# Hybrid decoder trunk: pooled projection in f32 with f32 band matmuls, x work as fine queued steps, SiLU phase moved up

## Chip, cores and metric

One Trainium2 chip, the program on all 8 cores, each with two of the 16 sequences. The time is the device time of the slowest core in microseconds (us), lower is better.

## Reference

```python
for l in range(2):                                  # x: (16, 2048, 1024) f32
    z = rms_norm(x, norm1_g[l]) @ w_in[l]           # 1792 columns, split over three mixers
    ya = silu(layer_norm(causal_dwconv31(a * sigmoid(gate)) + b)) @ w_pw[l]          # 384
    yb = u * (tril(w_s) @ layer_norm(v) + b_s)      # gelu, chunks of 128             # 384
    yc = ((trailing means over 2/4/8/16) - z_c) @ w_pool[l] * pool_scale[l]           # 256
    x = x + concat([ya, yb, yc]) @ w_out[l]
    gate, up = split(rms_norm(x, norm2_g[l]) @ w_gate_up[l], 2)                       # 2816 each
    x = x + (silu(gate) * up) @ w_down[l]
out = rms_norm(x, final_g)
```

## The kernel before

A core keeps one sequence of 2048 tokens as `xT`, 1024 features on 8 times 128 partitions, in f32. The tokens are cut into four blocks j of 512. A layer runs, on TensorE: `A` (the gated projection of mixer A, per block 8 groups of 8 matmuls 128x384), `V` and `U` (mixer B's projections), `conv`, then a loop over blocks with `U`, `ZB`, `SP`, `V`, `Z`, `TR`, `PT`, then the SiLU phase (`lnt`: 16 transposes of the normalised convolution output `xc` into a quad of four PSUM banks and four SiLU activations on ScalarE, for each of three channel tiles), then `WO` (output projection) and `FFN`, whose last chunk ends in a down projection of 32 groups of four matmuls 128x512, ordered by block.

The pooled mixer: `Z` projects each 128 tokens to 256 columns, ScalarE copies them scaled to bf16 (`zh`), VectorE writes what the rounding left (`zl`). `ZB` multiplies both with constant band matrices (`band`, `bandp` from the piece before, `bandc` at the sequence's start): for each of four windows six matmuls, seven in block 0. `PT` transposes the result.

Each engine takes its instructions in program order. Background work (norms, statistics, the convolution's Toeplitz tiles `toep`) is held as closures in the queues `bg`, `lo`, `nq` and `hq`; `tick` and `tick_n` pop some of them between foreground groups, and `need(tag)` pops until a tag is done. A norm (`norm_closures`) squares 8 tiles on ScalarE (`sqa`), adds them in pairs on VectorE (`sqr`), sums them on TensorE (`stat`, four matmuls 128x1 with `ocS`), and takes the power on GpSimd. In the kernel before it is six closures, and at the start of a layer also makes `xb`, the bf16 input of the projections. `x_tr` transposes a block of the staged input `xst` into `xT` (32 f32 transposes, 8 copies split over ScalarE and VectorE), and `fin_store` transposes a block back, scales it on VectorE (8 operations into `osA`, `osB` or `osF`) and stores it. Both are foreground code. Between the two sequences, every block goes through norm `rF`, `fin_store`, `x_tr`, norm `r1` and `A`; `pre` in the main loop sets that order.

Of the kernel before, what the change touches and what calls it, by code (L numbers as in the profile page):

```python
# [11 lines left out]
D = 1024  # L12
S = 2048
NT = 512
# [172 lines left out]
def build_program(nseq=2, depth=2):  # L187
# [51 lines left out]
    bt = alloc("bt", [128, 32], F32)  # L239
# [4 lines left out]
    w_pw = alloc("w_pw_sb", [128, 3, DA], BF16)  # L244
# [45 lines left out]
    y2 = AT("y2", 98304, [128, NBLK + 2, NG], BF16)  # L290
    silT = AT("silT", 98304, [128, 3, S], BF16)
# [16 lines left out]
    XSO = [45056, 61440, 77824, 61440]  # L308
    xstage = [[AT("xst%d_%d" % (j, q), XSO[j] + 4096 * q, [128, D], F32) for q in range(4)] for j in range(NJ)]
# [138 lines left out]
    def tick_n(n):  # L448
        for _ in range(n):
            if not hq or not pop_h():  # L450
                break
        if nq:
            pop(nq)
# [25 lines left out]
    def x_dma(s, j, eng="sync"):  # L479
        for q in range(4):  # L480
            tb = 4 * j + q
            dma(eng, xstage[j][q][:], x_d[s, tb * 128:(tb + 1) * 128, :], [], [xstage[j][q].b()])
# [5 lines left out]
    def load_w_rest(s, l):  # L488
# [3 lines left out]
        if s == 0:  # L492
            dma("gpsimd", w_pw[:], w_pw_d[l], [], [B("w_pw")])
# [14 lines left out]
    def load_wo(s, l):  # L508
        ha = [wo_b(0, 0), wo_b(0, 1)]
        hc = [wo_b(1, 0), wo_b(1, 1)]  # L510
        if s == 0:
            dma("gpsimd", woA[:, 0:3, :], w_out_d[l, :, 0:3, :], [], ha)
            dma("sync", wpf[:], w_pool_d[l], [], [wpf.b()])
# [6 lines left out]
    def fuse_a(h):  # L520
        hs = slice(512 * h, 512 * h + 512)
        got = []
        for ci in range(3):
            bk, bb = next_bank()
            mm(bk[:], [(w_pw[:, mk, ci * 128:(ci + 1) * 128], woA[:, mk, hs]) for mk in range(3)],
               [B("w_pw"), wo_b(0, h)], [bb])
# [60 lines left out]
    def band_consts():  # L587
        for g, w in enumerate((2, 4, 8, 16)):
            T = dF[:, 0, :]
# [10 lines left out]
            pool(lambda e: e.iota(bt[:], [[1, 32]], base=1, channel_multiplier=0,  # L600
                                  allow_small_or_imprecise_dtypes=True), [], [bC3])
# [3 lines left out]
            pool(lambda e: e.affine_select(out=bt[:], in_=bt[:], pattern=[[1, 32]], compare_op=ALU.is_ge, fill=0.0,  # L605
                                           base=0, channel_multiplier=-1), [bC3], [bC3])
            vec(lambda e, g=g: e.tensor_copy(out=bandc[:, 0, g, :], in_=bt[:]), [bC3], [bC3])
            tt(bandc[:, 1, g, :], bt[:], bandc[:, 0, g, :], ALU.subtract, [bC3], [bC3])
        pool(lambda e: e.memset(onesF[:], 1.0), [], [bC3])

    sq_rr = [0]

    def norm_closures(s, l, j, rt, kind, with_xb):
# [27 lines left out]
        def mkxb(k):  # L641
            if k % 2 == 0:
# [10 lines left out]
        def step(p):  # L653
            if p >= 2:
                stat(p - 2)
            if p < 4:
                for k in (2 * p, 2 * p + 1):
                    if with_xb:
                        mkxb(k)
                    sq(k)  # L660
            if 1 <= p <= 4:
                add(p - 1)
            if p == 5:
                fin()
        for p in range(6):
# [259 lines left out]
    def zb(tl, i, q):  # L925
        return tl[i].b(q, lo=512 * q, n=512)
# [321 lines left out]
```

How the kernel before makes its waits and increments, by code:

```python
                def body(eh):  # L165
                    for fn, waits, tok, dma in e.ops:
                        for k, v in waits:
                            eh.wait_ge(sems[k], v)
                        ins = fn(eh)
                        ins.then_inc(sems[tok[0]], 16 if dma else 1)
                    if e.name == "sync":
                        for k, v in finals:
                            eh.wait_ge(sems[k], v)
```

## Time and profile before

| | |
|---|---|
| runs | 2943.06 us median of 3 (2941.85 to 2948.37) |
| profiled execution | 2949.38 us, its span 2947.5 us on the slowest core |
| spans of the eight cores | 2935.0 to 2947.5 us |
| TensorE matmul busy | 2754.1 us, 93% of the span |
| VectorE, ScalarE, GpSimd busy | 1234.6, 794.5, 174.0 us |
| TensorE's share of the chain that ended last | 84% |
| an output tile, from issue to landing at the end | 2.9 us |

The busy share is a mean over stages that differ: in the FFN stages TensorE is busy without a gap, and its idle time lies in the start, between the two sequences, in the mixers and at the end. So what a change is worth is read stage by stage.

### The profile page before, as it was taken

The numbers are of one execution on the slowest core, as the hardware profiler recorded it, in microseconds if no ns is written. First come the engines' busy times: TensorE is split into PE (matmuls) and PEld (weight loads), VectorE is DVE, ScalarE is ACT, GpSimd is POOL, SyncE is SP. The second block draws the span as 40 slices with busy tenths as digits, with TensorE's granted clock in tenths as the row PEclk, the third lists the DMA queues.
The fourth block names the chain that finished last, engine by engine and source line by source line (L and its number), as shares of the span: only waits on it lengthen the run. The fifth ranks groups of instructions, "written<-read, shape, count | busy, mean of one in ns | idle before, by whom it ended". The sixth has DMA issues, their size and how long they took to land.

```text
span 2947.5 us, 42647 instructions; the slowest of 8 cores (2935.0 to 2947.5 us)
## 1 busy us (share of the span) xinstructions
PE 2754.1 (93%) x14860; PEld 1395.5 (47%) x14860; DVE 1234.6 (42%) x2256; ACT 794.5 (27%) x1360; POOL 174.0 (6%) x280
## 2 busy tenths in 40 slices
PE   4799999999998999999877899999999989999998
PEld 3554444444465344444455644444445644444444
DVE  2464431323664523323454653323335644323237
ACT  3554201011545311010244532010016442010102
POOL 3010100000000010000000001000000100000000
PEclk8799999999999999999978999999999999999999
DMA  8213342210123072121333026221002121121102
GB/s 189 39 35 58 51 71 51 36 30 15 31 51 69 1 116 36 29 50 22 95 129 76 17 44 93 46 44 36 15 16 54 26 51 36 29 51 36 36 15 115
DMA packets 124031, 150.35 MB, mean 51 GB/s; under 512 B 71728, under 2 KB 98224, under 8 KB 121776
## 3 DMA queue, kind: packets, MB, share of 16 engines
q0 software_dynamic: 36512, 97.33, 19.7%
q1 hardware_dynamic: 87312, 50.31, 6.1%
q8 instruction: 124, 2.03, 0.3%
q14 instruction: 83, 0.68, 0.1%
HBM read 215.05 MB, written 25.69 MB: 82 GB/s over the span
## 4 chain that ended last, share of the span: by engine, by line
PE 84%; DVE 6%; issue 3%; ACT 3%; DMA 2%; POOL 1%; SPq 1%; DVEq 0%; ACTq 0%; POOLq 0%
PE quad L346 78%; PE quad L364 2%; PE quad L793 2%; DVE h2T L397 1%; ACT sqa L375 1%; PE quad L963 1%; DMA yd<-ytok 1%; ACT silT L375 1%; DVE sqr L385 1%; SPq L338 1%; PE quad L787 1%; DVE xT L385 1%; PE quad L636 1%; DVE vg L397 0%; DVE ybt L397 0%
## 5 line engine op out<-in xcount | busy, mean ns | idle before, releaser
L346 PE MATMUL quad<-h2T,ring 128*128 128x512 bf16 x5632 | 1222.6, 379 | 0.0
L346 PEld LDWEIGHTS quad<-h2T,ring 128*128 128x128 bf16 x5632 | 549.7, 98 | 665.0 <-issue 7.7
L385 DVE TENSOR_TENSOR act<-tsil,quad 128x512 bf16<-128x512 f32 x352 | 241.8, 687 | 952.4 <-PE quad L346 932.5
L346 PE MATMUL quad<-act,wd 128*128 128x512 bf16 x2816 | 615.6, 379 | 0.4
L385 DVE TENSOR_TENSOR xT<-xT,quad 128x512 f32<-128x512 f32 x640 | 438.2, 686 | 418.0 <-PE quad L346 391.3
L375 ACT ACTIVATE tsil<-quad 128x512 f32<-128x512 f32 x352 | 210.0, 597 | 1478.1 <-PE quad L346 1466.7
L346 PEld LDWEIGHTS quad<-act,wd 128*128 128x128 bf16 x2816 | 272.4, 98 | 327.1 <-issue 4.1
L375 ACT ACTIVATE sqa<-xT 128x512 bf16<-128x512 f32 x320 | 186.3, 619 | 221.8 <-DVE sqr L385 188.3
L346 PE MATMUL quad<-w_uv_sb,xb 128*128 128x384 bf16 x1024 | 177.8, 333 | 7.4 <-DVE zl L397 6.4
L346 PE MATMUL quad<-w_a_sb,xb 128*128 128x384 bf16 x1024 | 180.7, 338 | 0.1
L346 PEld LDWEIGHTS quad<-w_uv_sb,xb 128*128 128x128 bf16 x1024 | 100.8, 100 | 77.8 <-issue 16.8
L346 PEld LDWEIGHTS quad<-w_a_sb,xb 128*128 128x128 bf16 x1024 | 101.0, 101 | 68.9 <-issue 9.5
L636 PE MATMUL quad<-ocS,sqr 128*128 128x1 bf16 x640 | 38.7, 164 | 94.2 <-DVE sqr L385 93.7
L346 PE MATMUL quad<-silT,woA 128*128 128x512 bf16 x384 | 104.9, 382 | 0.0
L636 PEld LDWEIGHTS quad<-ocS,sqr 128*128 128x128 bf16 x640 | 33.8, 98 | 139.3 <-issue 124.5
L338 POOL DMA_DIRECT2D ring<-w_gate_up x88 | 46.7, 533 | 863.9 <-PE quad L346 799.7
L397 DVE SCALAR_TENSOR_TENSOR h2T<-xT,pv,quad 128x512 bf16<-128x512 f32 x128 | 89.2, 740 | 4.5 <-PE quad L346 4.3
L397 DVE SCALAR_TENSOR_TENSOR ytok<-quad,r,sig 128x384 bf16<-128x384 f32 x64 | 39.5, 618 | 104.4 <-PE quad L346 87.6
L385 DVE TENSOR_TENSOR sqr<-sqa,sqa 128x512 bf16<-128x512 bf16 x160 | 66.7, 419 | 30.4 <-ACT sqa L375 27.3
L346 PE MATMUL quad<-yc,woA 128*128 128x512 bf16 x256 | 77.0, 383 | 0.0
L346 PE MATMUL quad<-ybT,woB 128*128 128x512 bf16 x256 | 76.9, 382 | 0.0
L650 POOL TENSOR_TENSOR r<-r,mhalf 128x4 f32<-128x4 f32 x32 | 32.6, 1017 | 621.3 <-DVE r L391 621.3
(126 smaller groups left out, 1730.8 us busy)
## 6 DMA issues: line engine op xcount, KB each, us to landing
ring<-w_gate_up POOLq DMA_DIRECT2D x88, 512.0 KB, 7.5
wd<-w_down POOLq DMA_DIRECT2D x12, 1536.0 KB, 12.1
xst<-x SPq DMA_DIRECT2D x24, 512.0 KB, 7.4
out<-osF SPq DMA_DIRECT2D x16, 512.0 KB, 2.9
w_a_sb<-w_a POOLq DMA_DIRECT2D x8, 768.0 KB, 23.2
w_uv_sb<-w_uv POOLq DMA_DIRECT2D x8, 768.0 KB, 33.4
yd<-ytok SPq DMA_DIRECT2D x16, 384.0 KB, 2.6
y<-yd SPq DMA_DIRECT2D x128, 48.0 KB, 2.8
```

The lines of the kernel that those rows point to most:

```text
L338: return P.add(q, lambda e, out=out, in_=in_: e.dma_start(out=out, in_=in_), reads=reads, writes=writes, dma=True, final=final)
L346: ins = e.matmul(out, l, r, start=(first and i == 0), stop=(last and i == n - 1))
L364: ins = e.transpose(out, in_, idn)
L375: return e.activation(out=out, in_=in_, func=func, **kw)
L385: return P.add(eng, lambda e, out=out, in0=in0, in1=in1, op=op: e.tensor_tensor(out=out, in0=in0, in1=in1, op=op), reads=reads, writes=writes)
L397: e.scalar_tensor_tensor(out=out, in0=in0, scalar=scalar, in1=in1, op0=op0, op1=op1),
L636: ins = e.matmul(bk[:, q:q + 1], sqr[p % 2][:, q * 128:(q + 1) * 128], ocS[:, 0:1], start=(p == 0 and q == 0), stop=(p == 3), skip_group_c ...
L650: pool(lambda e: e.tensor_tensor(out=rt[:, 4 * j:4 * j + 4], in0=rt[:, 4 * j:4 * j + 4], in1=mhalf[:, 0:4], op=ALU.pow), [br, bC], [br])
L787: e.matmul(bk[:], onesb[0:32, :], cb32[:, 32 * b:32 * b + 32].unsqueeze(2).to_broadcast([32, 32, TB]), start=True, stop=False, skip_group_ ...
L793: ins = e.matmul(bk[:, gp * 128:(gp + 1) * 128], y2[:, 2 - d:2 - d + NBLK, g], toep[:, g, d].rearrange("p i t -> p (i t)"), start=False, s ...
L963: ins = e.matmul(out, l_, r_, start=(n == 0), stop=(n == len(seq) - 1), skip_group_check=True)
```

## The change

Four edits, and moves of buffers that they need. (1) `Z` writes one f32 tile `zf` with a ScalarE copy, `zl` is gone, and `ZB` multiplies f32 by f32 band matrices: three matmuls per window in place of six or seven. (2) Norms are twelve closures in place of six; `x_tr`, `fin_store` and the loads of `x` become closures, which `tick(3)` pops in the last down projection and `A` pops with more ticks; at the start of the sequence the band constants' GpSimd part and VectorE part are apart, the latter after `A` of block 0. `osA` and `osB` have five buffers each. (3) The first `lnt` stands ahead of `TR` of the last block, and the last block's evictions go to VectorE. (4) The load of `w_pw` goes to after the convolution, and the loads of `sgB` to after `A` of block 3.

```diff
-    band = alloc("band", [128, 4, 128], BF16)
-    bandp = alloc("bandp", [128, 4, 32], BF16)
-    bandc = alloc("bandc", [128, 2, 4, 32], BF16)
+    band = alloc("band", [128, 4, 128], F32)
+    bandp = alloc("bandp", [128, 4, 32], F32)
+    bandc = alloc("bandc", [128, 4, 32], F32)
...
-    zh = [AT("zh%d" % i, 86016 + 4096 * i, [128, 4, DC], BF16) for i in range(2)]
-    zl = [AT("zl%d" % i, 88064 + 4096 * i, [128, 4, DC], BF16) for i in range(2)]
+    zf = [AT("zf%d" % i, 86016 + 4096 * i, [128, 4, DC], F32) for i in range(2)]
...
-    XSO = [45056, 61440, 77824, 61440]
+    XSO = [[45056, 61440, 77824, 61440], [45056, 61440, 45056, 61440]]
...
-    osA = [AT("osA%d" % i, 98304 + 4096 * i, [128, D], F32) for i in range(3)]
-    osB = [AT("osB%d" % i, 53248 + 4096 * i, [128, D], F32) for i in range(2)]
+    osA = [AT("osA%d" % i, o, [128, D], F32) for i, o in enumerate((114688, 118784, 122880, 86016, 90112))]
+    osB = [AT("osB%d" % i, o, [128, D], F32) for i, o in enumerate((77824, 81920, 86016, 90112, 104640))]
...
-    def tick_n(n):
+    def tick_n(n, m=3):
+        tn[0] += 1
+        for _ in range(m // 2 + (m % 2) * (tn[0] % 2)):
+            if nq:
+                pop(nq)
...
-            ts(bt[:], bt[:], float(w), None, ALU.min, None, [bC3], [bC3])
-            vec(lambda e: e.reciprocal(out=bt[:], in_=bt[:]), [bC3], [bC3])
-            ts(bt[:], bt[:], 1.0 / w, None, ALU.subtract, None, [bC3], [bC3])
...
+    def band_vec():
+        bb_ = B("bw")
+        for g, w in enumerate((2, 4, 8, 16)):
+            ts(bw[:, g, :], bw[:, g, :], float(w), None, ALU.min, None, [bb_], [bb_])
+        vec(lambda e: e.reciprocal(out=bw, in_=bw), [bb_], [bb_])
+        for g, w in enumerate((2, 4, 8, 16)):
+            ts(bw[:, g, :], bw[:, g, :], 1.0 / w, None, ALU.subtract, None, [bb_], [bb_])
...
+        def step(i):
+            if i >= 5 and i % 2 == 1:
+                stat((i - 5) // 2)
+            if i < 8:
+                if with_xb:
+                    mkxb(i)
+                sq(i)
+            if i >= 3 and i % 2 == 1 and i <= 9:
+                add((i - 3) // 2)
+            if i == 11:
                 fin()
+        for i in range(12):
+            push(lambda i=i: step(i), (kind, s, l, j) if i == 11 else None, nq if kind == "r2" else None)
...
+        for k in range(8):
+            push(lambda k=k: f(k))
...
+    def pre(s, j):
+        if s > 0:
+            fin_store(s - 1, j, osA if j < 2 else osB)
+        x_tr(s, j)
+        if s > 0 and j < 2:
+            push(lambda: x_dma(s, j + 2))
+        if s == 0 and j == 1:
+            push(lambda: x_dma(0, 3))
+        if j == 3:
+            push(lambda: None, ("x3", s))
+        norm_closures(s, 0, j, r1, "r1", True, s == 0 or j >= 2)
...
+    def evict(out, in_, reads, writes, j):
+        if j + 1 < NJ:
+            act_op(out, in_, AF.Copy, reads, writes)
+        else:
+            vec(lambda e: e.tensor_copy(out=out, in_=in_), reads, writes)
...
-            act_op(zh[i][:, q, :], bk[:, 0:DC], AF.Copy, [bb, br], [zb(zh, i, q)], scale=rc)
-            stt(zl[i][:, q, :], bk[:, 0:DC], rc, zh[i][:, q, :], ALU.mult, ALU.subtract, [bb, br, zb(zh, i, q)],
-                [zb(zl, i, q)])
+            act_op(zf[i][:, q, :], bk[:, 0:DC], AF.Copy, [bb, br], [zb(i, q)], scale=rc)
...
+                            if s + 1 == nseq:
+                                fin_store(s, j, osF)
+                            elif j < 2:
+                                pre(s + 1, j)
+                    tick(3 if l + 1 == L else 1)
...
+                if s == 0:
+                    pre(0, 0)
+                    need(("r1", 0, 0, 0))
+                    band_pool()
+                    pre(0, 1)
+                    A(s, l, 0, 2)
+                    band_vec()
+                    pre(0, 2)
+                    A(s, l, 1, 2)
+                    need(("r1", 0, 0, 2))
+                    pre(0, 3)
+                else:
+                    pre(s, 2)
+                    A(s, l, 0, 4)
+                    need(("r1", s, 0, 1))
                     load_conv(0)
...
+                if j + 1 == NJ:
+                    dma("gpsimd", woB[:], w_out_d[l, :, 6:8, :], [], [wo_b(3, 0)])
+                    pace[1], pace[2] = 1, 1
+                    lnt(s, l, 0)
                 TR(s, l, j)
                 if j > 0:
                     PT(s, l, j - 1)
...
+            lnt(s, l, 1)
             ZB(s, l, NJ - 1)
-            if s == 0:
-                fuse_c(l, 0)
-            lnt(s, l, 1)
+            lnt(s, l, 2)
             PT(s, l, NJ - 1)
```

On VectorE, at the start of the program: the copies of block 1 into `xT`, the band constants, and the norm of block 1 (`xb_73` before and `xb_71` now are that block's). Before:

```order
L676 COPY xT<-quad 128x512 x4
L391 TENSOR_SCALAR bt<-bt 128x32
L603 RECIPROCAL bt<-bt 128x32
L391 TENSOR_SCALAR bt<-bt 128x32
L607 CAST bandc<-bt 128x32
L385 TENSOR_TENSOR bandc<-bt,bandc 128x32
```

Three more such groups of five rows follow, and then:

```order
L391 TENSOR_SCALAR xb_73<-xT,pv 128x512 x2
L385 TENSOR_TENSOR sqr_59<-sqa_119,sqa_120 128x512
L391 TENSOR_SCALAR xb_73<-xT,pv 128x512
L385 TENSOR_TENSOR sqr_60<-sqa_121,sqa_122 128x512
```

Now:

```order
L396 SCALAR_TENSOR_TENSOR ytok_105<-quad,r_59,sig_108 128x384
L390 TENSOR_SCALAR xb_71<-xT,pv 128x512 x4
L384 TENSOR_TENSOR sqr_57<-sqa_116,sqa_117 128x512
L390 TENSOR_SCALAR xb_71<-xT,pv 128x512 x2
L384 TENSOR_TENSOR sqr_58<-sqa_118,sqa_119 128x512
L396 SCALAR_TENSOR_TENSOR ytok_105<-quad,r_59,sig_107 128x384
L390 TENSOR_SCALAR xb_71<-xT,pv 128x512 x2
L384 TENSOR_TENSOR sqr_57<-sqa_116,sqa_117 128x512
L384 TENSOR_TENSOR sqr_58<-sqa_118,sqa_119 128x512
L390 TENSOR_SCALAR r_59<-quad 128x4
L396 SCALAR_TENSOR_TENSOR ytok_105<-quad,r_59,sig_108 128x384
L390 TENSOR_SCALAR bandc<-bandc 128x32 x4
```

The norm of block 1 now stands among the outputs `ytok_105` of block 0's `A`, and ahead of the band constants.

On TensorE, in the last down projection of the first sequence (`act,wd` are its matmuls, `ocS,sqr` a norm's sums, `identF,xT` the transposes of `fin_store`). Before:

```order
L346 MATMUL quad<-act,wd_97 128x512 x8
L636 MATMUL quad<-ocS,sqr_60 128x1 x4
L346 MATMUL quad<-act,wd_97 128x512 x24
L636 MATMUL quad<-ocS,sqr_59 128x1 x4
L346 MATMUL quad<-act,wd_97 128x512 x8
```

Now:

```order
L345 MATMUL quad<-act,wd_95 128x512 x4
L644 MATMUL quad<-ocS,sqr_57 128x1 x4
L644 MATMUL quad<-ocS,sqr_58 128x1 x4
L345 MATMUL quad<-act,wd_95 128x512 x4
L363 MATMUL quad<-identF,xT 128x128 x12
L345 MATMUL quad<-act,wd_95 128x512 x4
L363 MATMUL quad<-identF,xT 128x128 x12
L345 MATMUL quad<-act,wd_95 128x512 x4
L363 MATMUL quad<-identF,xT 128x128 x8
L363 MATMUL quad<-identF,xst_0_0_141 128x128
```

The norm's sums stand closer together, and the transposes out and in stand between the groups of the down projection.

On TensorE, at the end of a mixer part (`identF,xc` are the transposes of `lnt`, `identb,ybt` is `TR`, `identb,pp` is `PT`, `zf,band` belongs to `ZB`). Before:

```order
L346 MATMUL quad<-w_z_sb,xb_75 128x256 x32
L364 MATMUL quad<-identb,ybt 128x128 x12
L364 MATMUL quad<-identb,pp 128x128 x8
L364 MATMUL quad<-identF,xc 128x128 x16
L963 MATMUL quad<-zh_99,band 128x256
L963 MATMUL quad<-zl_101,band 128x256
L963 MATMUL quad<-zh_99,bandp 32x192
L963 MATMUL quad<-zl_101,bandp 32x192
L963 MATMUL quad<-zh_98,bandp 32x64
L963 MATMUL quad<-zl_100,bandp 32x64
```

Now:

```order
L345 MATMUL quad<-w_z_sb,xb_73 128x256 x32
L363 MATMUL quad<-identF,xc 128x128 x16
L363 MATMUL quad<-identb,ybt 128x128 x12
L363 MATMUL quad<-identb,pp 128x128 x8
L363 MATMUL quad<-identF,xc 128x128 x16
L992 MATMUL quad<-zf_97,band 128x256
L992 MATMUL quad<-zf_97,bandp 32x192
L992 MATMUL quad<-zf_96,bandp 32x64
```

Two of the three SiLU transposes now stand ahead of the last `ZB`, and a window takes three matmuls.

## Rows read from the trace of the kernel before

**Rows 1.** Waits on TensorE, whole span: us in total, times, longest
```profile
PE quad L636 <- DVE sqr L385: 93.7, 70, 18.2
PE quad L364 <- DVE osB L397: 17.1, 2, 8.9
PE quad L364 <- ACT silT L375: 16.6, 8, 2.6
...
PE quad L963 <- DVE zl L397: 6.7, 4, 1.7
PE quad L346 <- DVE zl L397: 6.4, 6, 1.8
PE quad L787 <- DVE vg L397: 5.8, 1, 5.8
...
PE quad L364 <- DVE zl L397: 3.7, 2, 1.9
```

**Rows 2.** Busy us in four stretches: engines, granted clock, DMA share, GB/s
```profile
0.00:98.00 98.00, 47.42 (x323) 33.92 (x324) 33.51 (x80) 41.63 (x73) 23.29 (x66) 0.79 0.72 151
1431.80:1593.00 161.20, 119.30 (x771) 78.97 (x770) 85.92 (x160) 70.68 (x121) 9.38 (x11) 0.85 0.39 121
1431.80:1460.00 28.20, 28.10 (x159) 12.85 (x158) 23.76 (x42) 11.71 (x20) 1.26 (x2) 1.00 0.38 132
2919.00:2948.00 29.00, 16.22 (x153) 13.75 (x152) 24.39 (x42) 6.46 (x12) 2.01 (x2) 0.93 0.73 290
```

**Rows 3.** TensorE in order of time, first blocks: start, us [idle before <- releaser]
```profile
36.91 3.66 PE L364 MATMUL quad<-identF,xst 128*128 128x128 f32 x32
58.73 0.24 PE L636 MATMUL quad<-ocS,sqr 128*128 128x1 bf16 x4 [18.16 <-DVE sqr L385]
...
97.40 22.41 PE L346 MATMUL quad<-w_a_sb,xb 128*128 128x384 bf16 x128
119.65 10.56 PE L346 MATMUL quad<-w_uv_sb,xb 128*128 128x384 bf16 x64
```

**Rows 4.** VectorE by line: busy, mean ns | idle before it
```profile
L385 DVE TENSOR_TENSOR xT<-xT,quad 128x512 f32<-128x512 f32 x640 | 438.2, 686 | 418.0 <-PE quad L346 391.3 <-PE quad L636 25.2 <-issue 0.3
...
L385 DVE TENSOR_TENSOR sqr<-sqa,sqa 128x512 bf16<-128x512 bf16 x160 | 66.7, 419 | 30.4 <-ACT sqa L375 27.3 <-PE quad L636 1.3 <-ACT sig L375 1.2
L397 DVE SCALAR_TENSOR_TENSOR ytok<-quad,r,sig 128x384 bf16<-128x384 f32 x64 | 39.5, 618 | 104.4 <-PE quad L346 87.6 <-ACT toep L375 7.1 <-ACT sig L375 5.2
...
L391 DVE TENSOR_SCALAR xb<-xT,pv 128x512 bf16<-128x512 f32 x64 | 30.0, 479 | 0.1
L397 DVE SCALAR_TENSOR_TENSOR osF<-quad,rF,gFB 128x512 f32<-128x512 f32 x32 | 22.1, 743 | 0.4 <-PE quad L364 0.4
L676 DVE COPY xT<-quad 128x512 f32<-128x512 f32 x32 | 21.6, 688 | 22.5 <-PE quad L364 21.6 <-PE quad L636 0.9
...
L391 DVE TENSOR_SCALAR bt<-bt 128x32 f32<-128x32 f32 x8 | 1.4, 180 | 9.1 <-POOL bt L600 8.6
```

**Rows 5.** ScalarE by line, the squares of the norms
```profile
L375 ACT ACTIVATE sqa<-xT 128x512 bf16<-128x512 f32 x320 | 186.3, 619 | 221.8 <-DVE sqr L385 188.3 <-DVE xT L385 33.5
```

**Rows 6.** TensorE in order of time: a pooled product, then an f32 matmul
```profile
220.59 0.27 PE L963 MATMUL quad<-zh,band 128*128 128x256 bf16 x1
...
223.19 0.82 PE L346 MATMUL quad<-vn,wsT 128*128 128x384 bf16 x4
...
273.17 1.10 PE L346 MATMUL quad<-dF,onesF 128*128 128x512 f32 x2
274.11 0.38 PE L346 MATMUL quad<-ybT,woA 128*128 128x512 bf16 x1
```

**Rows 7.** Weight loads by form: busy, mean ns
```profile
L346 PEld LDWEIGHTS quad<-dF,onesF 128*128 128x128 f32 x32 | 4.8, 188 | 14.6 <-issue 14.6
```

**Rows 8.** TensorE in order of time, end of the first mixers
```profile
227.34 0.83 PE L364 MATMUL quad<-identb,ybt 128*128 128x128 bf16 x12
...
244.97 0.38 PE L346 MATMUL quad<-ybT,woA 128*128 128x512 bf16 x1 [1.24 <-ACT silT L375]
```

More of the change, by code:

```diff
@@ L512, in load_wo @@
             dma("gpsimd", woA[:, 0:3, :], w_out_d[l, :, 0:3, :], [], ha)
+            dma("gpsimd", w_pw[:], w_pw_d[l], [], [w_pw.b()])
             dma("sync", wpf[:], w_pool_d[l], [], [wpf.b()])
@@ L525, in fuse_a @@
             mm(bk[:], [(w_pw[:, mk, ci * 128:(ci + 1) * 128], woA[:, mk, hs]) for mk in range(3)],
-               [B("w_pw"), wo_b(0, h)], [bb])
+               [w_pw.b(), wo_b(0, h)], [bb])
             got.append((bk, bb))
@@ L651, in fin, with f @@
                                            in1=mhalf[:, 0:4], op=ALU.pow), [br, bC], [br])
[L653 to L663, printed above, removed]
+        def step(i):
[8 more added lines that the diff above has]
+            if i == 11:
                 fin()
-        for p in range(6):
-            push(lambda p=p: step(p), (kind, s, l, j) if p == 5 else None, nq if kind == "r2" else None)
+        for i in range(12):
+            push(lambda i=i: step(i), (kind, s, l, j) if i == 11 else None, nq if kind == "r2" else None)
     def x_tr(s, j):
-        for k in range(8):
+        xs = xstage[min(s, 1)][j]
+        def f(k):
             bk, bb = next_bank()
-            transposes([(bk[:, q * 128:(q + 1) * 128], xstage[j][q][:, k * 128:(k + 1) * 128], identF[:])
-                        for q in range(4)], [xstage[j][q].b() for q in range(4)] + [bC], [bb])
+            transposes([(bk[:, q * 128:(q + 1) * 128], xs[q][:, k * 128:(k + 1) * 128], identF[:])
+                        for q in range(4)], [xs[q].b() for q in range(4)] + [bC], [bb])
             if k % 2 == 0:
@@ L739, in A, with toep_closures @@
                 [byd], [y2b(j, i)])
-    def toep_closures():
+    def toep_closures(guard=None):
         gs = NG // 3
-        for part in range(3):
+        for part in ((2, 0, 1) if guard else (0, 1, 2)):
             for i in range(NI):
                 def f(part=part, i=i):
+                    if guard and part < 2:
+                        need(guard)
                     o = toep[:, part * gs:(part + 1) * gs, :, i, :]
@@ L964, in fn @@
                 return ins
-            rd = [zb(z, i, q) for z in (zh, zl) for q in range(4)]
+            rd = [zb(i, q) for q in range(4)] + [B("bw")]
             if j > 0:
-                rd += [zb(zh, 1 - i, 3), zb(zl, 1 - i, 3)]
+                rd += [zb(1 - i, 3)]
             P.add("tensor", fn, reads=rd + [bC3], writes=[bb])
-            act_op(pp[:, :, 128 * h:128 * h + 128].rearrange("p q (g c) -> p g q c", g=2),
-                   bk[:].rearrange("p (g q c) -> p g q c", g=2, q=4), AF.Copy, [bb], [pp.b()])
+            evict(pp[:, :, 128 * h:128 * h + 128].rearrange("p q (g c) -> p g q c", g=2),
+                  bk[:].rearrange("p (g q c) -> p g q c", g=2, q=4), [bb], [pp.b()], j)
             tick(1)
@@ L1129, in build_program @@
                     U(s, l, j)
+                    if s == 0 and j + 1 == NJ:
+                        fuse_c(l, 0)
+                        fuse_c(l, 1)
+                        keep_wo(l)
                     ZB(s, l, j - 1)
@@ L1168, in build_program @@
             FFN(s, l, after)
-    for j in range(NJ):
-        need(("rF", nseq - 1, L - 1, j))
-        fin_store(nseq - 1, j, osF)
+    drain()
     assert not bg and not lo and not nq and not hq
```

137 lines of the change are left out of this document (51 added, 86 removed).

## The prediction

> **What bounds the kernel now.** I began with the busy time in slices. In the FFN stages TensorE is busy without a gap, and nothing in the change touches their matmuls. So I went on to the waits on TensorE [rows 1]: 93.7 us for a norm's pair sums on VectorE (`sqr`), 17.1 for `osB`, 16.6 for SiLU outputs, and 16.8 (6.7, 6.4 and 3.7) put down to `zl`, the second bf16 part of the pooled projection. The windows [rows 2] say where. In the first 98 us TensorE is busy for 47.4, at a mean granted clock of 0.79. From 1431.8 us, where the last down projection of the first sequence begins, to 1593, where `A` of the next ends, it is busy for 119.3 of 161.2 us at 0.85: 30% of the time at the lower level (1.2 GHz), all of it after the first 28.2 us, which are gapless at 1.00. The last 29 us belong to VectorE, busy for 24.4. The change works at these three places and in the mixers, so the sum has four terms. In three of them TensorE is the engine that waits; in the last VectorE sets the end.
>
> **Start of the program.** The longest wait of all, 18.2 us, ends at 58.7 us [rows 3]. VectorE, in order, stands in the band constants there: `bt` alone waits 8.6 us for GpSimd [rows 4], because each window's constants go from one engine to the other and back. The norm of block 1 is queued behind them and TensorE behind the norm. Now those operations come after the norm and wait for GpSimd work long done. Blocks 1 to 3 also no longer go through transposes, norm and `A` one after another: they pass while TensorE has the `A` of the block before. `A` of block 0 ends at 36.9 us now, where block 1's transposes begin. From there TensorE's own work is 3 times 3.66 us of transposes and three `A` of 10.6 us (10.56 us for 64 matmuls of that shape at full clock), 42.7 us, and I add 5 us for the norms' 12 rounds of sums and their leftover waits: `A` of block 3 ends at 84.6 us in place of 119.8 (97.40 + 22.41). That is 35 us. The convolution then waits 5.8 us (the row that names `vg`), since the last `y` has to go through memory; its store no longer shares the SyncE queue's bandwidth with the `sgB` loads, which I count as 3 us. The loads of `sgB` come later for it, but what reads them on VectorE is followed on TensorE only after the convolution. Term: -38 us. Bounds: -28, if each of three norms keeps the 3 us of waits that a norm has when nothing stands between; -44, if the whole 5.8 and the norms' waits go. The later load of `w_pw` on GpSimd's queue waits for the convolution, and its reader is a loop pass further on; I cost it at nothing, and if it were late TensorE would stand in block 1 of the loop.
>
> **Between the sequences.** The down projection's 32 groups need 0.88 us each on TensorE (28.2/32) and 0.686 on VectorE [rows 4]. With three closures behind each, VectorE is the slower one there. Its work in that stage: 32 x 0.686 = 22.0 us, two norms `rF` with 8 x 0.419 = 3.4, one norm `r1` with four sums and four `xb`, 3.6, sixteen operations of `fin_store` at 0.743, 11.9, eight copies at 0.688, 5.5; together 46.4. I add 6 us in which it waits for a norm's end (the last squares on ScalarE, 0.62 each [rows 5], the sums on TensorE, the power on GpSimd, about 2 us, three times): 52.5 us where 28.2 stand now, so this stage gives back 24 us. Behind it: 7 half-groups of `A` beside two and a half norms, where ScalarE sets the pace (21 squares at 0.62, three `xb`, the sigmoids, 17.5 us); then 9 groups of `A` with 64 + 64 transposes, where VectorE does 16 x 0.743 + 8 x 0.688 + 16 x 0.479 + 8 x 0.419 + 5 x 0.618 = 31.6 us, with 2 of waits 33.6; then 16 groups of `A` alone, 21.1. The sum is 124.7 us, and I add 8 for what is left of waits and of the lower clock: 133 in place of 161.2. The stores and loads of `x` go out earlier, and with five output buffers the two waits of 17.1 us for `osB` are gone; the second sequence's block 2 is loaded into the place of block 0 and no longer waits for the down weights' place. Term: -28 us, bounds -10 and -42 (TensorE's own work is near 105 us, so some wait must stay).
>
> **Mixers.** Gone is `zl`: 30 us of VectorE and the 16.8 us of TensorE's waits for it, which I count in full, since the bank is now freed by ScalarE's copy. Added is the f32 product. A pooled product of four windows takes 2.60 us now (220.59 to 223.19), 0.65 per window and six matmuls [rows 6]. The only f32 matmul that isn't a transpose, 128x512, holds TensorE for 0.94 us (273.17 to 274.11). A window in f32 streams 256 + 192 + 64 = 512 columns, so 0.94 us is the lower bound. In bf16 it streams 1024 columns, 0.44 us at the rate of the down projection, so 0.21 us of the 0.65 is what small matmuls cost besides; half of it on top gives 1.05. The upper bound leaves each of six f32 weight loads uncovered at 188 ns [rows 7]: 1.98. I take 1.05, since the loads of the large product are mostly covered. There are 64 windows (16 calls of four), so +26 us, between +19 and +85. The SiLU phase: from `TR` of block 3 to `WO` 17.6 us pass now [rows 8]. Afterwards there are 48 f32 transposes (3.66/32 each, 5.5 us), 28 small ones, 1.6, `ZB` at its old price, 2.6, and one wait of about 2.4 between the first two SiLU tiles, which still share a quad: 12.1 us. Of the 5.5 saved about 0.9 is the four `fuse_c` matmuls of the first sequence, that only move. 4.6 x 4 = 18 us. The last block's evictions move 4 operations per layer from ScalarE to VectorE, which has the time of `zl` for them. Term: -17 - 18 + 26 = -9 us, bounds -20 and +50.
>
> Here a rule of the Trainium skill can be set beside the row. FP8 and Floating Point Precision, section TensorE Precision Notes, says that a true FP32 product takes four passes through the array; the row of 0.94 us against 0.22 us for the same shape in bf16 (4.3 times) agrees. By the rule alone a window would take 2048 columns' time, 0.88 us, and the product would cost +15 us in place of +26. It speaks against this edit: two bf16 parts take two passes.
>
> **End.** Now the down projection of 28.2 us is followed by 29.5 us of output work. Afterwards VectorE, already the limit, does it in one stretch: 7 us for the first eight groups, 24 x 0.686 = 16.5, three norms, 5.0, 24 x 0.743 = 17.8 and three waits of 2 for the norms' ends, 52.3; then for the last block a norm (4 us with its waits), 8 x 0.743 = 5.9 and the last tile's landing, near 3. Together 65 against 57.7. Some of the waits should overlap, so +6 us, bounds 0 and +9.
>
> **Sum.** -38 - 28 - 9 + 6 = -69 us on an execution of 2949.4 us (its span is 2947.5). That execution lies 6.3 us above the median of 2943.1, to which I apply the difference: 2874 us.
>
> **Rivals.** *The FFN's tail gives it all back.* If the waits of VectorE behind each norm are 4 us and not 2, and TensorE falls to the lower level meanwhile, the stage from 1431.8 us still takes 155: the term is -6 and the time 2896. For it: VectorE and TensorE are within 20% of each other there; against it: all of today's idle time lies behind that stage. *The f32 product costs its uncovered loads*: +85 in place of +26, 2933 us. Against it: the loads of the large f32 product are covered. *More is gained*: norms stop being waited for at the layer boundaries too, and the lower clock vanishes with the waits, 2845 us. *The other side, slower*: the product's clock. If the f32 windows ran at the lower level, one would take 4 passes at half rate, 1.9 us, and six uncovered loads, 3.0 us together; 64 x (3.0 - 0.65) = +150 us would leave +55, 2998 us. It decides from 2.1 us per window on, where it eats the other terms' 95 us. Against it: TensorE is busy through the mixers, and nothing in the trace drops the clock without a wait. That the change does nothing can't be: the rows of the three places differ in the program order.
>
> **Chances.** Forecast 0.62 (2855 to 2890), the tail 0.16, uncovered loads 0.07, more gained 0.12, slower 0.03. The range reaches from most of the fourth case to the second: 2838 to 2904, and leaves 2 in 10 out. Within 0.2% (6 us, what a measurement of this kernel can just tell) of the old time I see 0.01, slower 0.03, faster 0.96.
>
> **What would show it.** `A` of block 3 ends near 85 us and no wait near 18 us is left. The stretch that began at 1431.8 us lasts 133 us, its down projection over 50. A window of `ZB` takes 1.05 us. `TR` to `WO` takes about 14 us with the dearer `ZB`. The last down projection's first matmul to the end takes over 60. I am wrong if the three norms in the FFN's tail hold TensorE for long, or if a window takes over 1.3 us.

## The result and the profile after

The changed kernel takes 2920.39 us, the median of five runs, against 2948.18 for the kernel before in the same comparison (2915.83 to 2921.71 and 2941.85 to 2948.37, each without one disturbed run, of 3303.66 and 3254.18, that the comparison leaves out). The ratio is 0.9914, with a 95% interval of 0.9898 to 0.9931. It is faster, by 0.9% where 2.3% were forecast, and 2920 lies outside the range of 2838 to 2904.

The profiled execution has a span of 2918.8 us on its slowest core. What TensorE waits for in it, on that core (us in total, times, longest):

```profile
PE quad L644 <- DVE sqr L384: 60.3, 67, 3.4
PE quad L345 <- ACT dF L374: 35.1, 16, 3.5
PE quad L363 <- ACT silT L374: 14.6, 4, 3.7
PE quad L363 <- DMA xst<-x: 14.2, 2, 12.0
PE quad L816 <- DMA sgB<-sg_ln_g: 7.8, 3, 3.3
```

Against [rows 1] the `osB` and `zl` waits are gone and the sums' waits are a third shorter. The second line is new in its size. The broadcast of the second norm (`dF`) was waited for in 4 places for 6.8 us, and is now in all 16 for 35.1. The last line is the wait in front of the convolutions: its matmul reads no `sgB`, but `y`, which comes back from memory through the same SyncE queue. The windows that answer to [rows 2] (engine busy us, then granted clock, DMA share, GB/s):

```profile
0.00:98.00 98.00, 70.36 (x485) 47.92 (x486) 48.81 (x114) 48.63 (x80) 23.31 (x61) 0.95 0.76 161
1409.70:1545.00 135.30, 110.71 (x772) 72.08 (x771) 91.33 (x181) 69.37 (x117) 9.46 (x11) 0.94 0.46 145
1409.70:1461.50 51.80, 45.50 (x305) 28.23 (x304) 41.76 (x75) 21.43 (x38) 3.05 (x3) 0.97 0.52 198
```

In the first 98 us TensorE is busy for 70 in place of 47. The stretch from the last down projection of the first sequence to the end of the next `A` is 135.3 us, and the down projection in it 51.8; the clock there rose from 0.85 to 0.94.

A single core's span differs from another's by up to 15 us. So from here on stages are compared by their mean over all eight cores of the profiled execution. A stage begins with the first TensorE matmul of its kind. "Lower clock" is the stage's length times one less its granted clock, "idle" the time in which TensorE has no matmul.

| stage | before: us, lower clock, idle | after | forecast | change |
|---|---|---|---|---|
| start to first convolution | 134.2, 23.6, 54.4 | 104.6, 4.7, 30.1 | -38 | -29.7 |
| last down projection of sequence 1 to convolution | 169.1, 22.6, 41.2 | 147.4, 9.4, 26.1 | -28 | -21.7 |
| convolution to `WO`, four layers | 408.1, 19.1, 46.1 | 405.4, 15.1, 18.5 | -9 | -2.6 |
| last down projection to the end | 59.3, 2.4, 13.4 | 65.2, 3.6, 17.7 | +6 | +5.9 |
| `WO` and FFN to the last down projection, four layers | 1991.4, 3.8, 28.6 | 2009.7, 7.9, 44.1 | none | +18.3 |
| the two boundaries between layers | 178.6, 0.0, 12.1 | 177.5, 0.0, 11.4 | none | -1.1 |
| all | 2940.7, 71.5, 195.8 | 2909.8, 40.7, 148.0 | -69 | -30.9 |

The row with no forecast is the largest miss: 18 of the 38 us that are lacking.

### The profile page after: what moved, and what is told of

It is laid out like the page before. It is cut to its first block, busy times and chain, and to the rows that moved or that the text cites. A ratio compares the mean times of both kernels' runs of the same rounds, so it can differ in the third digit from the quotient of the medians.

```text
span 2918.8 us, 42424 instructions; the slowest of 8 cores (2903.2 to 2918.8 us)
## 1 busy us (share of the span) xinstructions
PE 2770.4 (95%) x14844; PEld 1410.5 (48%) x14844; DVE 1222.0 (42%) x2225; ACT 766.0 (26%) x1316; POOL 173.6 (6%) x274
## 4 chain that ended last, share of the span: by engine, by line
PE 87%; DVE 4%; issue 3%; ACT 2%; DMA 2%; POOL 1%; SPq 1%; DVEq 0%; ACTq 0%; POOLq 0%
PE quad L345 79%; PE quad L363 3%; PE quad L992 3%; PE quad L822 2%; DVE sqr L384 1%; DVE xT L384 1%; ACT sqa L374 1%; DVE h2T L396 1%; DMA xst<-x 1%; PE quad L816 1%; ACT dF L374 1%; POOL r L658 1%; PE quad L644 1%; SPq L337 1%; DMA sgB<-sg_ln_g 0%
## 5 line engine op out<-in xcount | busy, mean ns | idle before, releaser
L345 PEld LDWEIGHTS quad<-h2T,ring 128*128 128x128 bf16 x5632 | 550.9, 98 | 668.2 <-issue 11.4
L345 PE MATMUL quad<-w_uv_sb,xb 128*128 128x384 bf16 x1024 | 171.0, 326 | 0.0
L384 DVE TENSOR_TENSOR sqr<-sqa,sqa 128x512 bf16<-128x512 bf16 x160 | 66.5, 422 | 28.5 <-ACT sqa L374 27.7
```

Of the source, the lines that this page charges most:

```text
L345: ins = e.matmul(out, l, r, start=(first and i == 0), stop=(last and i == n - 1))
L384: return P.add(eng, lambda e, out=out, in0=in0, in1=in1, op=op: e.tensor_tensor(out=out, in0=in0, in1=in1, op=op), reads=reads, writes=writes)
```

## Experiments

The number behind each kernel is the mean span of the eight cores in its profiled execution (before 2940.7, after 2909.8). One core's span scatters by 5 to 7 us, so a mean over eight by some 2; executions of one kernel have means 2 to 5 us apart (2908.0 to 2910.1 for the changed one, 2884.2 to 2889.2 for `c1_best`). So two kernels can be told apart from about 5 us on, and smaller differences are read from the stages.

**The order of the queues.** In the changed kernel `tick_n` pops the norm's own queue first:

```diff
-        for _ in range(m // 2 + (m % 2) * (tn[0] % 2)):
-            if nq:
-                pop(nq)
         for _ in range(n):
             if not hq or not pop_h():
                 break
+        for _ in range(m // 2 + (m % 2) * (tn[0] % 2)):
+            if nq:
+                pop(nq)
```

> The changed kernel with one edit: tick_n pops the queue hq (the steps of the second norm's broadcast) before the queue nq (the norm's own steps), as the kernel before did. Theory (order of the queues): with nq first, the norm's last closure and the steps dia, no-op and bc fall into one tick, so the broadcast's matmul stands right behind the norm's last sums, and TensorE waits 35.1 us in 16 places for dF. Then the dF waits fall to about 7 us (6.8 before), each stretch from the first gate matmul to the last down projection falls from 439.3 to about 435 us, and the time from 2920 to about 2897 us. Rival (pace): the FFN stages are longer because the norm now has twelve steps at up to two per tick, beside which VectorE and ScalarE are late; then the dF waits move to sqr and the time stays within 5 us of 2920.

Measured: 2902.2, so 8 us less. The `dF` waits fell to 14.1 us in 8 places, not to 7, and the sums' waits rose:

```profile
PE quad L644 <- DVE sqr L384: 74.9, 79, 3.4
PE quad L345 <- ACT dF L374: 14.1, 8, 2.0
```

`WO` and FFN took 499.5 us per layer, in the changed kernel 502.4 and before 497.9. The order is a cause, but not the whole. (The expectation of e6_rate below has 499.3 us here and 13 us still lacking over four layers. That is an error of mine: the stages give 6.5.) The opposite edit, on the kernel before, is the sharper test:

```diff
     def tick_n(n):
+        if nq:
+            pop(nq)
         for _ in range(n):
             if not hq or not pop_h():
                 break
-        if nq:
-            pop(nq)
```

> The kernel before with one edit: tick_n pops nq before hq. Theory (order of the queues): the broadcast's matmul comes right behind the norm's last sums, TensorE waits for dF some 16 times, about 28 us in all in place of 6.8, and the time rises from 2948 to about 2970 us; each layer's stretch from the output projection to the last down projection takes 5 to 7 us more. Rival (e1_order gave back only 8 us): the sum waits get shorter by as much as the dF waits grow, and the time rises by no more than 8 us.

Measured: 2956.5, 15.8 us more, ratio 1.0113 (1.0061 to 1.0165). Its waits:

```profile
PE quad L636 <- DVE sqr L385: 78.4, 60, 18.1
PE quad L346 <- ACT dF L375: 35.2, 16, 3.5
```

One swapped pair of lines makes all 16 waits. About half of the 28 us is given back by the sums, whose waits fell by 15. Each `WO` takes 3.2 us more (66.7 against 63.5), each FFN 1.0. The profiled execution is the shortest of the four behind the ratio: their mean spans go from 2956.5 to 2967.7, 20.9 us above those of the kernel before in the mean (2963.7 against 2942.8). So the swap costs 16 to 21 us, nearer to the theory than to the rival.

**The norm's pace.** Besides the order, the norm of twelve steps went at one and a half steps per tick in `WO`, which is slower than six steps at one per tick. On top of the edit of e1_order:

```diff
-    def tick_n(n, m=3):
+    def tick_n(n, m=4):
```

> The changed kernel with tick_n popping hq before nq, as in e1_order, and with two steps of the second norm per tick in the output projection too (m=4 in place of 3): a norm of twelve steps then takes six ticks everywhere, the pace of the kernel before. By the means over the eight cores, e1_order lost its waits for dF in part only (14 us of 35) and the stage from the output projection to the last down projection stayed 13 us above that of before over four layers (499.3 against 497.9 us per layer in the mean, 498 to 500). Theory (order and pace together): the dF waits fall to about 7 us, TensorE's idle time in the stretch from the first gate matmul to the last down projection falls from 7 to about 4.3 us, that stretch from 438 to 435 us, and the time by 10 us more than in e1_order, to about 2905. Rival (neither, but what stands beside the norm's matmuls: sum waits because the pair sums on VectorE come one step ahead): e6_rate is as e1_order, 2915, within 3 us in the mean over cores.

Measured: 2893.7, ratio 0.9826 (0.9795 to 0.9857). The `dF` waits are 7.1 us in 5 places, the first gate matmul to the last down projection takes 434.9 us and its idle time 4.3. This execution took 2902.76 us, which lies inside the range of the prediction, at its edge. With the second norm in six steps and one per tick, order and pace are those of the kernel before:

> The changed kernel with the second norm of a layer in six steps again, one per tick, and hq popped before nq: exactly the order of the kernel before in the output projection and the FFN; everything else as changed. Theory: the FFN's 18 us over four layers come from these edits and from nothing else, so the stretch from the output projection to the last down projection returns to 498 us per layer (502.3 now) and the mean span of the cores falls from 2910 to about 2892 us, the time to about 2902. Rival: the FFN is longer for another reason (the lower clock, or transfers that moved), then e7_six is as e1_order, 2915.

Measured: 2893.3 and 498.1 us per layer. The two agree, and `WO` and FFN are back at the 497.9 us of before within 0.2. So the 18 us are explained: order and pace, and nothing else in the change.

**The end.** The first attempt left `fin_store` as closures, pushed behind the last norm, and gave the last down projection one `tick(2)` per two groups in place of a `tick(3)` for each:

```diff
-                            if s + 1 == nseq:
-                                fin_store(s, j, osF)
...
-                    tick(3 if l + 1 == L else 1)
+                    if l + 1 == L and s + 1 == nseq:
+                        if n % 2 == 1:
+                            tick(2)
+                    else:
+                        tick(3 if l + 1 == L else 1)
...
+    for j in range(NJ):
+        need(("rF", nseq - 1, L - 1, j))
+        fin_store(nseq - 1, j, osF)
```

> The changed kernel with the end of the program as before: in the last down projection of the last sequence only the norms run, and fin_store of all blocks comes after it. Theory (VectorE sets the end, and the output work in the down projection takes nothing off it but adds waits): the last down projection's first matmul to the end falls from 65.1 to about 58.5 us, the time to about 2914. Rival: the stretch is as long in either order, 2920 within 2 us.

Measured: 2915.3, the end 65.8 us. But all output work now stood behind all norms, which is not the order of before, so it tells nothing of that order. With the output steps as foreground code and `tick(2)` behind each:

> The changed kernel with the end of the program in the order of before: the norms behind the last down projection, then, block by block, the eight output steps as foreground with a norm step pair behind each. In e4_end the output steps had been queued behind the last norm, which was not the order of before, and its end took 65.8 us. Theory (VectorE sets the end; output work inside the down projection only adds its waits there): the stretch from the last down projection to the end takes 59 us as before and not 65, and the time falls by 6 us to 2914. Rival: the six us come from the finer norm steps, then the end stays at 65.

Measured: 2906.1, the end 59.0 us, as the theory had it. VectorE is busy for 48.8 us of the end in the changed kernel and for 49.5 here, so the 6 us are its waits and not its work. But that output work inside the down projection is what costs isn't shown: e4_end took all of it out as well. Its down projection is 29.0 us long, as here and before (49.1 in the changed kernel), but what follows took 36.8 us, where it is 30.0 here. What gives the 6 us back is the order of before as a whole: each block's output outside the down projection, with the next block's norm between its steps.

**The f32 product.** `zh`, `zl` and bf16 bands again:

```diff
-                    seq = [(o, band[:, g, :], zf[i][:, :, gc]),
-                           (o[0:32, 1:4, :], bandp[:, g, :], zf[i][:, 0:3, gc])]
+                    seq = [(o, band[:, g, :], zh[i][:, :, gc]), (o, band[:, g, :], zl[i][:, :, gc]),
+                           (o[0:32, 1:4, :], bandp[:, g, :], zh[i][:, 0:3, gc]),
+                           (o[0:32, 1:4, :], bandp[:, g, :], zl[i][:, 0:3, gc])]
```

> The changed kernel with the pooled projection in two bf16 parts and bf16 bands again (zh, zl, bandc in two parts); all else stays. Theory (the product costs what its windows measured, 1.18 us against 0.65): TensorE's pooled products get shorter by 64 x 0.53 = 34 us, some of the 17 us of zl waits come back, and the time falls by 20 to 30 us, to 2890 to 2900. Rival A: the zl waits come back in full and a little more, because VectorE now also has the last block's evictions; then it falls by 10 or less, to 2910 or above. Rival B (what I forecast, 1.05 us and 16.8 us of waits): by 9, 2911.

Measured: 2915.4, 5.6 us more and not 20 to 30 less. A stretch of the first mixers shows why, in this kernel and then in the changed one, both on core 0 (busy us of TensorE first; granted clock third from the end):

```profile
105.00:190.00 85.00, 78.42 (x589) 51.83 (x590) 55.46 (x137) 40.56 (x71) 9.25 (x11) 0.92 0.17 37
```

```profile
105.00:190.00 85.00, 84.80 (x633) 57.18 (x634) 52.37 (x129) 44.43 (x78) 9.25 (x11) 0.98 0.22 42
```

From the convolution to `WO` over four layers TensorE idles for 42.8 us and not 18.5, and loses 23.7 and not 15.1 us to the lower clock. So 24 us of idle time and 9 of clock stand against the 34 us by which the windows are shorter. On the slowest core the profile names `zl` for 17.0 us of the waits, as much as in the kernel before. Whether that holds where other waits are gone was tried on the best kernel below:

> c2_late with the pooled projection in two bf16 parts again. Theory (the f32 product costs 34 us in its windows, and saves as much because the waits for zl, about 24 us of idle TensorE, bring some 10 us of lower granted clock): mean span 2853 + 0 to 5 us. Rival A (with the norms' waits gone the lower clock doesn't come, so the bf16 version wins): 10 us faster, 2843. Rival B (VectorE is the tighter engine now): slower by 10 or more.

Measured: 2859.0 against 2853.2. From the convolution to `WO` TensorE idles for 42.6 us and not 18.8, and loses 29.1 and not 16.8 us to the lower clock. It holds: the f32 product costs nothing net here, and gains perhaps 3 to 6 us (the other executions have mean spans of 2854.5 and 2857.2 with bf16, and 2853.1 to 2854.6 with f32).

**The SiLU phase.** Back behind `TR` and `PT`, evictions on ScalarE:

```diff
-                    lnt(s, l, 0)
                 TR(s, l, j)
...
-            lnt(s, l, 1)
+            lnt(s, l, 0)
             ZB(s, l, NJ - 1)
-            lnt(s, l, 2)
+            lnt(s, l, 1)
             PT(s, l, NJ - 1)
+            lnt(s, l, 2)
```

> The changed kernel with the SiLU phase where it was: the first lnt behind TR and PT, then ZB of the last block, lnt, PT, lnt, and the last block's evictions on ScalarE. Theory (the SiLU phase did give its gain, 4 us per layer, though the f32 product hid it): the time rises by 12 to 18 us, to 2932 to 2938. Rival: it gave next to nothing, because the second lnt still waits for the first one's SiLU on the same quad and for an activation table load; then the time stays within 4 us of 2920.

Measured: 2911.5, from the convolution to `WO` 402.6 us against 405.4. On top of the two repairs:

> As c1_best, but with the SiLU phase and the last block's evictions as before (the edit of e3_silu). Theory (e3_silu: the move gained nothing, the stretch from convolution to output projection was 402.6 us in the sum over four layers against 405.4 with it): mean span 2885, within 3 us of c1_best. Rival (my forecast of 18 us for the move): 2900 or more.

Measured: 2882.7 against 2886.8; other executions of the two lie at 2879.3 to 2897.5 and 2884.2 to 2889.2, so they can't be told apart. Twice the move bought nothing. The changed kernel on ScalarE and then on TensorE shows the reason (start, us; in brackets the idle time before and what ended it):

```profile
192.82 1.28 ACT L374 ACT_TABLE_LOAD   x1 [1.75 <-PE quad L363]
194.11 2.79 ACT L374 ACTIVATE silT<-quad,pv 128x512 bf16<-128x512 f32 x4
```

```profile
190.33 1.91 PE L363 MATMUL quad<-identF,xc 128*128 128x128 f32 x16
192.08 0.83 PE L363 MATMUL quad<-identb,ybt 128*128 128x128 bf16 x12
192.75 0.61 PE L363 MATMUL quad<-identb,pp 128*128 128x128 bf16 x8
197.04 3.32 PE L363 MATMUL quad<-identF,xc 128*128 128x128 f32 x16 [3.69 <-ACT silT L374]
```

The second tile's transposes need the first tile's quad, and so wait for a table load of 1.28 us and four SiLUs of 2.79. Only `TR` and `PT`, 1.3 us, stand between, and 3.7 us are idle time. Before, `ZB` stood at that place, and another wait came ahead of the third tile (TensorE of the kernel before):

```profile
235.18 1.94 PE L364 MATMUL quad<-identF,xc 128*128 128x128 f32 x16 [1.76 <-ACT silT L375]
...
240.20 3.53 PE L364 MATMUL quad<-identF,xc 128*128 128x128 f32 x16 [2.21 <-ACT silT L375]
```

So the move took `ZB` from one wait to cover another. With the 0.8 us ahead of `WO` (1.2 before) TensorE idles for 4.5 us between the first `lnt` and `WO` of the first layer now, for 5.3 before and for 4.2 in e3_silu, where the longer f32 `ZB` stands at the old place. Behind the wait comes the lower clock: the 16 transposes take 3.32 us and not 1.91, in this stretch of the changed kernel (granted clock third from the end):

```profile
197.00:200.40 3.40, 3.36 (x17) 3.39 (x18) 0.00 (x0) 0.81 (x1) 0.00 (x0) 0.56 0.00 0
```

**The start.** I had put the 18.2 us wait down to the band constants on VectorE. Its rows in the kernel before show them, first and last, 16.0 us apart with nothing else between:

```profile
41.28 0.17 DVE L391 TENSOR_SCALAR bt<-bt 128x32 f32<-128x32 f32 x1
...
57.13 0.19 DVE L385 TENSOR_TENSOR bandc<-bt,bandc 128x32 bf16<-128x32 f32 x1
```

One edit on the kernel before:

```diff
-                    band_consts()
                     A(s, l, 1)
+                    band_consts()
```

> The kernel before with one edit: band_consts() stands behind the second A in place of ahead of it, nothing else. Theory (as the prediction had it: the 18.2 us wait is VectorE standing in the band constants, the rest of the start's gain is the interleaving): the 18.2 us wait falls to about 8, the stretch from the first A to the convolution from 108.8 to about 99 us. Rival A: it was the whole of the gain, the stretch falls to about 82 as in the changed kernel. Rival B: block 1's transposes and norm alone make that wait, it stays above 15 us.

Measured: 2938.5, ratio 1.0016 (0.9976 to 1.0056), and the stretch 107.9: no change. The wait of 18.2 fell to 3.1, and a new one came (TensorE of this kernel; the 9.3 us that is now its longest wait for `sqr` lies between the sequences and was 9.6 before):

```profile
45.35 0.25 PE L636 MATMUL quad<-ocS,sqr 128*128 128x1 bf16 x4 [3.05 <-DVE sqr L385]
...
80.49 1.94 PE L364 MATMUL quad<-identF,xst 128*128 128x128 f32 x8 [10.37 <-DVE xT L676]
```

The constants hold VectorE for as long wherever they stand, and what is behind them is merely another block's copies. In the changed kernel the constants need one instruction of GpSimd. There, early or late:

```diff
                     band_pool()
+                    band_vec()
                     pre(0, 1)
                     A(s, l, 0, 2)
-                    band_vec()
```

> The changed kernel with band_vec() right behind band_pool(), ahead of block 1's copies and norm on VectorE, where the constants stood in the kernel before. Theory (the waits came from nine round trips between VectorE and GpSimd, not from the place): VectorE's operations now need only GpSimd's first instruction, so the stretch from the first A to the convolution stays at 81 us within 2. Rival (the place counts): VectorE stands behind GpSimd's masks for up to 8 us and the stretch rises to 86 or more.

Measured: 80.8 us for the stretch against 81.1. The place doesn't count for the constants as they are now. And the interleaving undone:

```diff
-                    pre(0, 1)
-                    A(s, l, 0, 2)
+                    A(s, l, 0)
+                    pre(0, 1)
+                    need(("r1", 0, 0, 1))
                     band_vec()
+                    A(s, l, 1)
                     pre(0, 2)
-                    A(s, l, 1, 2)
-                    need(("r1", 0, 0, 2))
                     pre(0, 3)
+                    need(("r1", 0, 0, 3))
```

> The changed kernel with the start's blocks one after another again: transposes, norm, then A, for blocks 1 and then 2 and 3, each norm awaited ahead of its A; the constants as changed. Theory (both edits count): 9 us of the gain are VectorE's waits for GpSimd, the interleaving is worth the other 18, so the stretch from the first A to the convolution rises from 81 to about 98 us, the mean span from 2910 to 2927. Rival A (the interleaving is all): it rises to 108. Rival B (the constants are all): it stays below 86.

Measured: 92.7 us. Of the 27.7 us between 108.8 and 81.1, 11.6 are the interleaving's, and 16.1 are left. They are as long as the constants held VectorE, and the wait ahead of block 1's first sum, 18.2 us before, is 3.0 here. No run has the old constants in the changed kernel, so that the other edits at the start gave nothing is read from these rows and not tested. Without the interleaving there are 5.4 us more of idle time and 9.1 more of lower clock (12.6 against 3.5); part of the lower clock falls into the idle time, so the two together are more than the 11.6.

**Towards a better kernel.** The repairs together:

> The changed kernel with e6_rate's two edits (hq before nq, norm pace of before) and e4b_end's (the end in the order of before). Theory (the two repairs are at different places and add): mean span of the cores 2910 - 16 - 6 = 2888 us, the time about 2896, ratio to before 0.980. Rival (the end's gain is lost when the norms are late or early otherwise): no better than e6_rate, mean 2894, time 2902.

Measured: 2886.8, median 2900.23, ratio 0.9803 (0.9773 to 0.9833). The two repairs add. The largest group of waits left is that of the norms' sums, so the sums were put one pair later, with a third `sqr` buffer and two more steps per norm:

```diff
-            if i >= 5 and i % 2 == 1:
-                stat((i - 5) // 2)
+            if i >= 7 and i % 2 == 1:
+                stat((i - 7) // 2)
```

> As c1_best, but every norm's sum on TensorE comes one pair later (14 steps, three sqr buffers in place of two). 73 us of waits for sqr are left in e6_rate, the largest group, 1 to 1.9 us at a time. Theory (the sums wait because only one step lies between a pair sum on VectorE and its matmul): they halve, to about 35 us, the start (first A to convolution) falls from 81 to about 77 and the stretch between the sequences from 148 to about 142 us, the mean span from 2888 to about 2865. Rival (ScalarE's eight squares of 0.62 us set the pace of a norm, so that the sums wait for them wherever they stand, since need pops until the norm is done): unchanged within 4 us.

Measured: 2853.2, median 2862.94, ratio 0.9682 (0.9654 to 0.9709), the fastest of all. More than expected:

```profile
PE quad L644 <- DVE sqr L384: 38.7, 48, 3.5
```

`WO` went from 63.1 to 59.0 us in each layer, with 0.2 us of idle time left of 2.9, and the stretch between the sequences from 147.4 to 140.2. Of the 33.6 us between the two kernels 27.6 are idle time (129.1 against 101.5) and 2.9 lower clock. The rival doesn't hold: ScalarE's squares are no limit in most places, and the distance of one step was what the sums waited for. The third buffer is no rival: in c1_best the pair sums on VectorE idle for 26.6 us, 26.5 of them for ScalarE, so none for a buffer. At the start, where `need` pops the norm in one go, the gain is 1.4 us only, where 4 were expected.

## Why the prediction was wrong

- **The step that failed is the one that isn't in it.** My sum has terms for the start, the sequences, the mixers and the end; of the second norm I said nothing, although the diff shows `tick_n` with its two loops exchanged and a slower pace. I had put it at nothing without a reason, and it cost 18.3 us. Row by row in the changed kernel, for the first block (power on GpSimd, four scalings on ScalarE, broadcast on TensorE):

```profile
237.43 1.03 POOL L658 TENSOR_TENSOR r<-r,mhalf 128x4 f32<-128x4 f32 x1 [26.21 <-DVE r L390]
...
238.55 1.28 ACT L374 ACTIVATE dF<-identF,r 128x128 f32<-128x128 f32 x4 [6.92 <-POOL r L658]
...
239.97 1.10 PE L345 MATMUL quad<-dF,onesF 128*128 128x512 f32 x2 [1.74 <-ACT dF L374]
```

  From the last sum (236.24) to the broadcast 3.7 us pass, and the sum and one group of `WO`, 2.0 us together, cover half of them. With `hq` first another group stands between. The slower pace moves the broadcasts back: in the first layer the third one comes behind the first gate matmul, where it stood ahead of it before. So `WO` is 0.8 us shorter per layer than before (62.7 against 63.5) and the FFN 5.4 longer.
  The prediction's signs of being wrong named the norms in the FFN's tail and the window, and not this place.
- **Start, -38 forecast, -29.7.** `A` of block 3 ended at 92.2 and not 84.6. No wait near 18 us is left. From the first matmul of `A` at 23.9 us to that end TensorE idles for 10.4 of 68.3 us, 2.2 of it for `xst` and the rest for the norms' sums, where I had allowed 5 with the sums' own time; and the first 15.4 us run at a clock of 0.80, which costs 3 more. My 3 us for the wait in front of the convolution aren't there either: I took its 5.8 us from the slowest core, and in the mean over the eight it was 2.9 us and is 2.5. My mechanism for the 18.2 us (VectorE stands in the constants) was right, but "now those operations come after the norm" is not what removed it: in s1_consts they come ahead of it, and nothing changes.
- **Between the sequences, -28 forecast, -21.7.** The stage sums held: 51.8 us for the down projection (52.5 forecast), 135.3 for the whole (133). There is luck in the first: VectorE's operations are those I counted, but back to back they overlap and keep it busy for 41.8 us, not 46.4, and its waits are 10.0 us and not 6. Most of the rest is that I compared with the slowest core of before: 172.1 us there up to the convolution, 169.1 in the mean.
- **Mixers, -9 forecast, -2.6**, with errors that cancel in part. The window of `ZB` takes 1.18 us:

```profile
201.56 0.70 PE L992 MATMUL quad<-zf,band 128*128 128x256 f32 x2
202.19 0.62 PE L992 MATMUL quad<-zf,bandp 128*32 128x192 f32 x4
202.75 0.70 PE L992 MATMUL quad<-zf,band 128*128 128x256 f32 x2
```

  So the product costs 64 x 0.53 = 34 us and not 26. Each f32 matmul is recorded as two instructions, so a window still has six, and the 0.21 us that I took for what small matmuls cost besides seems to come in full on top of 0.94 (1.15), not by half; no run parts it from a part of the loads left uncovered. By the Trainium skill (FP8 and Floating Point Precision, TensorE Precision Notes), whose four passes gave 0.88 us, the sum would have missed by more; the trace doesn't agree at this size. Nearly all of the loads stayed covered, as I had it. (The upper bound of 1.98 us should have been 2.07, 0.94 and six times 0.188, and the price in that rival 91 us.) The `zl` waits were worth 33 us with the clock and not 17. The SiLU phase's 18 us weren't there: from the first `lnt` to `WO` 18.0 us pass (190.33 to 208.32), where `TR` to `WO` was to fall from 17.6 to about 14. The wait that I had at 2.4 us is 3.7, another 0.8 stands ahead of `WO`, and the clock behind the wait, of which I had nothing, costs 1.4 us in the transposes alone.
- **End, +6 forecast, +5.9.** Right: 49.1 and 16.2 us in the mean (52.3 and 13 forecast), and e4b_end takes it back. Why VectorE waits more there is open, as e4_end shows.
- **The rivals.** None came true. The tail didn't give the gain back, the loads weren't uncovered, and the product ran at full clock, but for the first window behind a wait (0.80).

The missing 38 us are 18 in `WO` and FFN, 8 at the start, 6 between the sequences and 6 in the mixers.

## What to carry to other kernels

Where a scheduler's pop order changes, list every wait that the order had covered, in the stages that the change doesn't mean too: here the swapped loops and the new pace cost 18 us of the 49 that the rest of the change had won. Ask of a moved block what wait it covered where it stood: `ZB` left one SiLU wait open to close another. A moved block of work that holds an in-order engine moves its wait along; look at what stands behind it at the new place. And a step's distance to its consumer is worth more than its size: one pair of steps more between the sums on VectorE and their matmuls gave 34 us, more than the whole change.

## What the runs showed of the hardware

- Short waits on TensorE cost more than their length in the mixers: with the `zl` waits back, 24 us of idle time came with 9 us more of lower granted clock. Behind one wait of 3.7 us the granted clock was 0.56 over 3.4 us, and 16 transposes took 3.32 us in place of 1.91.
- A small f32 matmul is recorded as two instructions and costs more than its columns: 0.63 us for 128x256, where the rate of the 128x512 one (0.94) gives 0.47. The weight loads of `band` take 197 ns each, and TensorE shows no idle time in a window.
- Eight cores with the same program differed by 15 us in one execution, with the granted clock between 0.983 and 0.988 in the profiled execution after the change, the longest at the lowest clock.
